# One more weight place, used once, ahead of the expert stages of a transformer kernel

## The reference, cut to what matters

```python
def second_block(x, mem, ...):
    h = x
    for layer in range(2):
        mix = mixer_ab(h, ...) if layer % 2 == 0 else mla(h, ...)
        h = layer_norm_2(DN_ALPHA * h + mix, ...)
        xa = mem_cross_attention(h, mem, xa_wq[layer], xa_wkv[layer], xa_wo[layer])
        h = layer_norm_2(DN_ALPHA * h + xa, ...)
        ff = hier_moe(h, ...)          # 32 experts in 4 groups, 2 chosen per token
        h = layer_norm_2(DN_ALPHA * h + ff, ...)
    return h

def expert_block(args):                # one block of rows of one expert e
    xb, e = args
    h = jax.nn.silu(xb @ w_gate[e]) * (xb @ w_up[e])   # 1024 -> 512
    return h @ w_down[e]                               # 512 -> 1024
```

## Time and profile before

| | |
|---|---|
| median of 3 runs | 2828.98 us (2827.93 to 2829.49) |
| profiled execution | 2828.16 us |
| its span | 2826.3 us, 38195 instructions |
| PE busy | 2510.8 us (89%), 16194 matmuls |
| DVE, ACT, POOL busy | 44%, 13%, 7% |
| DMA | 703.59 MB, mean 249 GB/s |
| mean granted TensorE clock | 0.952 |

### The profile page before, as it was taken

The page is one execution under the profiler, slowest core; times in us unless marked ns, Lnnn a source line. Parts: engine busy times, 40 slices in busy tenths (PEclk is TensorE's granted clock), DMA queues, the critical chain, the costliest instruction groups (busy, mean ns, idle before and its releaser), DMA issues.

```text
span 2826.3 us, 38195 instructions
## 1 busy us (share of the span) xinstructions
PE 2510.8 (89%) x16194; PEld 1656.4 (59%) x16194; DVE 1256.4 (44%) x2583; ACT 379.0 (13%) x865; POOL 210.5 (7%) x224
## 2 busy tenths in 40 slices
PE   9999999999999999999999999866667999756665
PEld 5779765796769947699457785322223675322221
DVE  4767664676666656777556532000002553000002
ACT  1410002100031001310022111000000412000000
POOL 0300012000120000400013000000000310000000
PEclk9999999999999999999999999988889999988888
DMA  8354543544535435254431868999999447999998
GB/s 322 120 161 156 190 145 120 189 157 161 193 106 178 176 116 205 89 190 170 143 128 49 297 244 343 421 421 421 421 421 386 182 185 304 421 421 421 421 422 340
DMA packets 245774, 703.59 MB, mean 249 GB/s; under 512 B 18795, under 2 KB 123753, under 8 KB 197219
## 3 DMA queue, kind: packets, MB, share of 16 engines
q1 hardware_dynamic: 244304, 699.30, 65.5%
q10 hardware_dynamic: 1299, 1.83, 0.2%
HBM read 698.20 MB, written 1.05 MB: 247 GB/s over the span
## 4 chain that ended last, share of the span: by engine, by line
PE 73%; DMA 21%; SPq 2%; ACT 2%; DVE 1%; issue 1%; DVEq 0%; ACTq 0%
PE lin L928 45%; PE sco L928 16%; PE trp L928 9%; DMA ring<-in_moe_w_down 5%; DMA ring<-in_moe_w_gate 5%; DMA arena<-in_moe_w_down 3%; DMA arena<-in_moe_w_up 2%; DMA arena<-in_moe_w_gate 2%; DMA ring<-in_moe_w_up 1%; PE trp L1097 1%; SPq L760 1%; DMA x<-in_moe_w_up 1%; DMA spare<-in_moe_w_gate 1%; PE trp L1193 1%; DMA x<-in_moe_w_down 1%
## 5 line engine op out<-in xcount | busy, mean ns | idle before, releaser
L928 PE MATMUL sco<-arena 128*32 128x512 f32 (+6 forms) x2560 | 551.5, 509 | 115.3 <-DMA ring<-in_moe_w_up 27.1
L928 PE MATMUL lin<-ring,arena 128*128 128x512 f32 (+3 forms) x1820 | 646.7, 504 | 2.6 <-DMA ring<-in_w_in_a 1.8
L928 PE MATMUL sco<-ring,arena 128*32 128x512 f32 (+2 forms) x1652 | 390.8, 690 | 136.6 <-DMA arena<-in_moe_w_up 39.2
L928 PEld LDWEIGHTS lin<-ring,arena 128*128 128x128 f32 x1820 | 339.0, 190 | 264.1 <-issue 238.6
L928 PEld LDWEIGHTS sco<-arena 128*32 128x32 f32 (+3 forms) x2560 | 201.5, 150 | 283.2 <-issue 271.2
L928 PE MATMUL lin<-arena 128*128 128x128 f32 (+8 forms) x2888 | 355.2, 300 | 3.6 <-ACT arena L2372 1.3
L3794 DVE TENSOR_TENSOR arena<-arena,sco 128x512 f32<-128x512 f32 x16 | 11.0, 687 | 758.1 <-PE sco L928 758.1
L928 PEld LDWEIGHTS lin<-arena 128*128 128x128 f32 (+3 forms) x2888 | 274.9, 170 | 63.1 <-issue 42.7
L928 PEld LDWEIGHTS sco<-ring,arena 128*32 128x32 f32 (+1 forms) x1652 | 107.3, 133 | 282.2 <-issue 275.3
L928 PE MATMUL trp<-arena 128*128 128x128 f32 (+2 forms) x1584 | 217.7, 292 | 1.3 <-ACT arena L2559 0.7
L2856 POOL TENSOR_TENSOR roots<-roots 128x1 f32<-128x1 f32 (+2 forms) x42 | 38.8, 926 | 2270.9 <-DVE roots L2981 2248.4
(11 more groups left out here) (366 smaller groups left out, 2369.1 us busy)
## 6 DMA issues: line engine op xcount, KB each, us to landing
ring<-in_w_gate_up SPq DMA_DIRECT2D x88, 1024.0 KB, 5.6
ring<-in_moe_w_up SPq DMA_DIRECT2D x66, 1024.0 KB, 26.7
ring<-in_moe_w_down SPq DMA_DIRECT2D x65, 1024.0 KB, 27.0
ring<-in_moe_w_gate SPq DMA_DIRECT2D x61, 1024.0 KB, 26.7
arena<-in_moe_w_gate SPq DMA_DIRECT2D x54, 1024.0 KB, 26.7
arena<-in_moe_w_up SPq DMA_DIRECT2D x51, 1024.0 KB, 26.5
arena<-in_moe_w_down SPq DMA_DIRECT2D x47, 1024.0 KB, 26.7
ring<-in_w_down SPq DMA_DIRECT2D x44, 1024.0 KB, 5.4
```

The costliest lines, as they stand in the source:

```text
L928: return nc.tensor.matmul(o, lhsT, rhs, start=start, stop=stop, skip_group_check=not one_group)
```

## The change

A further place, ONCE_PLACE, is used for a single piece in each expert stage, piece 7 (the last of the second four gate pieces of the first round). It consists of 1536 floats of the arena, over `pair_h`, `pair_hT` and more that is first written later in the first round, and of the 512 floats of the causal mask. In `expert_slots` it is put in at position 7, so every place behind it takes a piece one later. In `load_moe` it is loaded as two transfers into one semaphore, and out of order: directly ahead of the piece for TURNED_PLACE, with the same wait on `pv_full`. Behind layer 0's pieces the mask is loaded again from HBM (256 KB), and DVE waits for that ahead of the attention of the second layer. The unread products take the identity, repeated four times, as moving operand. Some of the router's tables move over `rowsT`, `hot` shares its place with `chosen`, and `gathering` and all that is behind it move; `moe_x` and the extra places start 32 floats further on, and the arena is 32 floats longer.

```diff
+ONCE_PIECE = 2 * TOGETHER - 1
...
+        once.insert(ONCE_PIECE, ONCE_PLACE)
         count = ROUNDS * PIECES + 2 * len(EARLY_MEMORY)
     else:
-        once = []
         cycle = (free + [MEMORY_PLACE] + oldest[0:4] + SUMS_PLACES + oldest[4:6] + [KEYS_PLACE, VALUES_PLACE, TURNED_PLACE] + oldest[6:10]
                  + [MIXED_PLACE] + oldest[10:11] + [COLUMNS_PLACE] + oldest[11:] + [X_PLACE])
+        once = cycle[:ONCE_PIECE] + [ONCE_PLACE] + cycle[ONCE_PIECE:]
...
+def load_order(slots):
+
+    order = [m for m in range(len(slots)) if m != ONCE_PIECE]
+    order.insert(order.index(slots.index(TURNED_PLACE)), ONCE_PIECE)
+    return order
...
-        ARENA = 25600
+        ARENA = 25632
...
-        PAIR = GATE + 512
+        PAIR = GATE + 288
         rowsT = at(PAIR, KD, P)
+        logits36 = at(PAIR, NT, GROUPS + EXPERTS)
...
+        once_rows = [at(PAIR + 1024 + 512 * n, 512) for n in range(3)] + [causal[:, :, :].rearrange("p t k -> p (t k)")]
-        gathering = at(PAIR + 2304, NT, P)
-        moe_x = at(PAIR + 2560, NT, 2, 4, P)
-        turned_rows = at(PAIR + 2560 + NT * D, SLOT)
+        gathering = at(PAIR + 2560, NT, P)
+        moe_x = at(PAIR + 2816, NT, 2, 4, P)
+        turned_rows = at(PAIR + 2816 + NT * D, SLOT)
...
-                for m, src in enumerate(sources()):
-                    s = slots[m]
+                matrices = list(sources())
+                for m in load_order(slots):
+                    s, src = slots[m], matrices[m]
...
-                    elif s == TURNED_PLACE or s == VALUES_PLACE and layer:
+                    elif s in (TURNED_PLACE, ONCE_PLACE) or s == VALUES_PLACE and layer:
                         sp.wait_ge(pv_full, 2 * XA_HEADS * (layer + 1))
+                    if s == ONCE_PLACE:
+                        sp.dma_start(at(PAIR + 1024, 3, 512), src[:, 0:3, :]).then_inc(slot_full[s], 16)
+                        sp.dma_start(once_rows[3], src[:, 3, :]).then_inc(slot_full[s], 16)
+                        continue
...
                 for s, dst, src in last_halves:
                     sp.dma_start(dst, src).then_inc(slot_full[s], 16)
+                if values_ahead(layer):
+                    sp.wait_ge(slots_used, before + ONCE_PIECE + 1)
+                    sp.dma_start(causal[:, :, :].rearrange("p t k -> p (t k)"), const("causal")).then_inc(causal_loaded, 16)
...
             def busy_work():
 
                 for n in range(4 + 2 + 1):
-                    mm(lin[:, 0, :], ident[:, :], causal[:, :, :].rearrange("p t k -> p (t k)"))
+                    mm(lin[:, 0, :], ident[:, :], ident[:, :].unsqueeze(1).to_broadcast([P, 4, P]))
...
                     for _ in range(TOGETHER):
                         s = next(next_slot)
+                        if s == ONCE_PLACE:
+                            pe.wait_ge(slot_full[s], full[s].next(32))
+                            parts.append(once_rows)
+                            continue
...
+                dve.wait_ge(causal_loaded, 16)
                 attend_pairs([causal] * (MLA_HEADS // 2), range(KD))
```

More of the change, by code:

```diff
@@ L69 @@
 (VALUES_PLACE, MEMORY_PLACE, KEYS_PLACE, X_PLACE, COLUMNS_PLACE, TURNED_PLACE,
- MIXED_PLACE) = [RING + EXPERT_EXTRA + n for n in range(7)]
+ MIXED_PLACE, ONCE_PLACE) = [RING + EXPERT_EXTRA + n for n in range(8)]
+ONCE_PIECE = 2 * TOGETHER - 1
 SUMS_PLACES = [RING + EXPERT_EXTRA - 2, RING + EXPERT_EXTRA - 1]
@@ L106, in expert_slots @@
     assert taken[MIXED_PLACE] < count - 2 * TOGETHER
+    assert taken[ONCE_PLACE] == ONCE_PIECE
     return places, earlier
+def load_order(slots):
+    order = [m for m in range(len(slots)) if m != ONCE_PIECE]
+    order.insert(order.index(slots.index(TURNED_PLACE)), ONCE_PIECE)
+    return order
 FFN_UNITS = D_FF // (2 * P)
@@ L317, in build @@
         late_row_sums = at(0, 2, 2, 512)
-        first_head_sums = at(ARENA - 880, 2, 3, P)
+        first_head_sums = at(ARENA - 912, 2, 3, P)
         mla_row_sums = at(14592, 8, 512)
@@ L347, in build @@
         chosen = at(GATE + 128, NT, COLUMNS)
+        hot = at(GATE + 128, NT, EXPERTS)
         numbers = at(GATE + 192, EXPERTS)
[L349 to L357, removed]
-        PAIR = GATE + 512
-        rowsT = at(PAIR, KD, P)
+        router = at(GATE + 224, NT, 16)
+        most = at(GATE + 256, 8)
+        PAIR = GATE + 288
+        rowsT = at(PAIR, KD, P)
+        logits36 = at(PAIR, NT, GROUPS + EXPERTS)
+        late_gates = at(PAIR, NT, EXPERTS)
+        picked = at(PAIR + 72, NT, GROUPS, PER_GROUP)
+        group_hot = at(PAIR + 136, NT, GROUPS)
+        group8 = at(PAIR + 144, NT, 8)
+        top8 = at(PAIR + 160, NT, 8)
+        group_exps = at(PAIR + 176, NT, GROUPS)
         pair_h = at(PAIR + 1024, MOE_FF)
@@ L364, in build @@
         spreadT = at(PAIR + 2048, NT, P)
-        gathering = at(PAIR + 2304, NT, P)
-        moe_x = at(PAIR + 2560, NT, 2, 4, P)
-        turned_rows = at(PAIR + 2560 + NT * D, SLOT)
+        once_rows = [at(PAIR + 1024 + 512 * n, 512) for n in range(3)] + [causal[:, :, :].rearrange("p t k -> p (t k)")]
+        gathering = at(PAIR + 2560, NT, P)
+        moe_x = at(PAIR + 2816, NT, 2, 4, P)
+        turned_rows = at(PAIR + 2816 + NT * D, SLOT)
         moe_sum = at(2048, NT, D)
-        EXTRA = PAIR + 2560 + NT * D + SLOT
+        EXTRA = PAIR + 2816 + NT * D + SLOT
         extra = at(EXTRA, EXPERT_EXTRA, SLOT)
@@ L459, in build @@
         sco = psum("sco", 2)
-        slot_full = [sem(f"slot_full{s}") for s in range(MIXED_PLACE + 1)]
+        slot_full = [sem(f"slot_full{s}") for s in range(ONCE_PLACE + 1)]
         slots_used = sem("slots_used")
@@ L491, in build @@
         x_ordered, columns_read = sem("x_ordered"), sem("columns_read")
+        causal_loaded = sem("causal_loaded")
         first_half_loaded = sem("first_half_loaded")
@@ L2004, in expert_parts @@
                         s = next(next_slot)
+                        if s == ONCE_PLACE:
+                            pe.wait_ge(slot_full[s], full[s].next(32))
+                            parts.append(once_rows)
+                            continue
                         pe.wait_ge(slot_full[s], full[s].next(16))
-                        parts.append(slot_rows(s).rearrange("p (k n) -> p k n", k=k))
+                        rows = slot_rows(s).rearrange("p (k n) -> p k n", k=k)
+                        parts.append([rows[:, j, :] for j in range(k)])
                     return parts
@@ L2042, in unread @@
                     for _ in range(n):
-                        mm(trp[:, 0, :], ident[:, :], causal[:, :, :].rearrange("p t k -> p (t k)"))
+                        mm(trp[:, 0, :], ident[:, :], ident[:, :].unsqueeze(1).to_broadcast([P, 4, P]))
                 def combine(n, i):
@@ L2076, in moe @@
                                 for r, wk in zip(expert_rows, parts):
-                                    last = mm(sco[r, gate_or_up, :], rowsT[:, 4 * half + k, r], wk[:, k, :],
+                                    last = mm(sco[r, gate_or_up, :], rowsT[:, 4 * half + k, r], wk[k],
                                               start=half + k == 0, stop=half == 1 and k == 3)
@@ L2100, in moe @@
                                 for r, wd in zip(expert_rows, parts):
-                                    last = mm(sco[r, n, :], pair_hT[:, 2 * half + f, r], wd[:, f, n * 512:(n + 1) * 512],
+                                    last = mm(sco[r, n, :], pair_hT[:, 2 * half + f, r], wd[f][:, n * 512:(n + 1) * 512],
                                               start=half + f == 0, stop=half + f == 2)
@@ L2666, in moe @@
                     act.wait_ge(vec_for_act, t_vec.next())
-                    nc.scalar.activation(hot[:, t, 0:GROUPS], logits36[:, t, 0:GROUPS], ACT.Exp, bias=router[:, t, 8:9],
+                    nc.scalar.activation(group_exps[:, t, :], logits36[:, t, 0:GROUPS], ACT.Exp, bias=router[:, t, 8:9],
                                          accum_out=router[:, t, 9:10])
```

## The result

The changed kernel takes 2813.44 us (median of 6 runs, 2811.46 to 2816.73), the one before 2829.23 (6 runs, 2825.44 to 2831.2): a ratio of 0.995, interval 0.9939 to 0.996. That is 15.8 us less (11 to 17 by the interval), where 5.0 were forecast. The profiled execution's span is 2809.6 us, 16.7 shorter.

The account below looks back on a forecast made before the run. Expert stages end paced by the 421 GB/s weight stream, the rest is PE-bound; -4.98 for the lead plus 0 each for mask, fillers and tables/arena/router takes 2828.98 to 2824.0 us, range 2822.2 to 2827.4.

Parts of the forecast that it names:

- The lead of one MB: Both expert stages: the new place puts one MB more ahead, so each ends 2.49 us earlier, -4.98 us in sum.
- B: Expert stages: one keeps its MB, the other gives it back as its queue runs dry once; 2826.5 us, chance 0.09.
- C: Expert stages: neither keeps its MB of lead; 2829.0 us, chance 0.04.
- D: Expert stages: a MB is worth more than the mean, 3.18 us at 330 GB/s; 2822.6 us, chance 0.11.
- The mask's load: Behind layer 0's stage: the 256 KB reload takes 0.68 us, within 1.9 us of slack; 0 taken, 0 to +0.9 kept.
- The fillers: Unread products ahead of layer 1's stage and in the tails: repeated identity as fast as the mask, 592 ns a pass; 0.
- E: Unread products: the repeated identity costs double, +7.7 us, so the kernel is slower at 2831.7 us; chance 0.05.
- Tables, arena, router ... I take 0: Router tables move with the same operations; expert buffers behind and spare start 128 bytes later, loads land alike; 0 us.
- Rival F: Stage loads into the arena: the 128-byte shift lowers their rate, 384 for 421 GB/s, +36.5 us; 2860.5 us, chance 0.04.

## Why the prediction was wrong, point by point

**The lead of one MB: right.** By the cuts of the stages, the changed kernel against the same without the place is 473.52 against 476.48 and 460.26 against 462.48: -2.96 and -2.22. The pair with all buffers moved is 471.29 against 474.04 and 459.37 against 461.33: -2.75 and -1.96. The mean over both pairs is -4.95 for both stages; -4.98 was worked out. The third pair, the kernel without the shift against before, gives -0.74 and -2.42, the first of them with the 1.6 us of a fallen clock in it. That neither stage gives it back was right too (rivals B and C are out). The shortest time from issue to landing behind the early memory products, named as the test, after and without the place:

```profile
DMA to landing us min/median/max: 9.5/10.6/11.6
```

```profile
DMA to landing us min/median/max: 12.0/13.0/14.1
```

2.5 us apart, the price of a MB, and still above the 5.6 of a lone load. (The forecast had 10.9 for the shortest, from the 13.4 of before.) A MB was worth its mean, so D is out as well.

**The mask's load: right.** The memory weights were issued at 2149.49, landed 11.8 us later at 2161.3, and PE read them at 2162.48: 1.2 us of slack, the 1.9 less the 0.68 worked out. DVE never waited for the mask; it landed 10.5 us after its issue at 2147.8, and its first reader starts at 2227.7.

**The fillers: right**, 592 ns a pass in the changed kernel too, so E is out:

```profile
L951 PE MATMUL lin<-ident x14: 592/592/676, 2361.3 to 2372.2; 128*128 128x512 f32 x14
```

**The step that failed is "Tables, arena, router ... I take 0".** The prediction saw that the places behind the gathered rows, and spare, move by 128 bytes, and priced it at nothing since loads into ring and arena "which start at different offsets, land alike". That comparison was worth nothing, for two reasons. First, by the count above, both buffers started 128 bytes past a multiple of 256, as did x and spare: there was no buffer of the other kind to compare with. An offset within the program is not an address in the partition; one must add up all that is allocated ahead of it. Second, 26 to 27 us from issue to landing in a full queue is the length of the queue, some ten transfers of others, and doesn't show the price of one's own. Even at 427 GB/s that median is 26.8 us within layer 0's stage, against 27.3 before. What the runs showed instead: the shift alone is worth 3.4 us in each stage, and 6.9 us in the median (0.9973).

Rival F named this very mechanism, with 0.04, but looked only at a loss. It also counted all 152 MB of loads into the arena, though those into mixT, xT and memT don't move and those into spare do. For a change of address, nothing in the trace excluded a gain, and the forecast gave no lower bound for it, as it did for the other unknowns. With -7 as that bound, the range would have reached down to 2817. The two effects' sum is -5.0 and -6.9, -11.9, which lies within the interval of the result and is close to the 12.2 us found in the stages. The 3.9 us from there to the median's -15.8 aren't shown by any run: against the before measured beside each, the kernel without the place is 8.4 us faster and the one without the shift 6.4, and the medians of before themselves lie between 2827.1 and 2829.2. They are likely scatter between executions.

**The mechanism of the address: open.** That the starts make the rate is shown, by moves alone. How they do isn't. Worked out from the traces' packet records, before rounding, the rates in GB/s of the two windows are these, beside what they would be if each place on a multiple of 256 gave its own share of the rise from 421.2 to 426.7 and 426.8:

| kernel | places on a multiple of 256, layers 0 and 1 | measured | by shares |
|---|---|---|---|
| before | 0 of 22, 0 of 25 | 421.2, 421.2 | |
| only spare moved (one run) | 0 of 22, 2 of 25 | 421.2, 422.1 | 421.2, 421.7 |
| nothing but the shift | 7 of 22, 9 of 25 | 424.3, 424.8 | 422.9, 423.2 |
| ring and x alone | 13 of 22, 13 of 25 | 426.5, 425.9 | 424.4, 424.1 |
| all moved | 22 of 22, 25 of 25 | 426.7, 426.8 | |

The gain is well above the share wherever only some places are moved. A move helps the loads of its neighbours in the stream too, or a start off the multiple costs more among others of its kind. "Each place by its own start", which stands in several expectations, is refuted.

The Trainium skill, "DMA: Bandwidth & Descriptors", section "How a descriptor splits into AXI transactions", says that each transaction into which a transfer is split, of 256 bytes or less, must start on a multiple of 256, and that the bytes between that boundary and the true start are fetched unused and cost beats of 32 bytes. Its table has small pieces only. By the rule a row of 8 KB costs 256 beats on a boundary and 260 from 128 bytes past one, 1.6% more: an estimate. In the mean these runs are near it: 426.7 against 421.2 is 1.3%. In the rest they don't agree. A start 64 past would cost 258 beats and one 192 past 262, so the far places would have moved the rate to some 422.3 and 420.1, both estimates; the runs have 421.1 to 421.2 for either. A count for each row gives plain shares, which the table above doesn't show. And it would lengthen every row: before, 4726 of the 18482 packets of 8192 bytes in layer 0's window took 309 ns, with a mean of 313.9, and with all moved 18697 of 18723 took 309 ns. The section speaks of bytes that are fetched, and here only the places that are written moved. The prediction weighed the same page's limit of the HBM and not this section; its estimate would have turned a zero into a term of the right sign.

## What to carry to other kernels

Where a stage runs at the full rate of its DMAs, look up the byte at which each buffer starts within the partition. Here a start on a multiple of 256 bytes for rows of 8 KB was worth 1.3% of the stream, for no instruction at all: 2828 to 2814 us with one unused line of 32 floats, about as much as the whole change, of which the new place alone gave some 5. One more buffer ahead of such a stage was worth its bytes over the stream's rate, and can be where it is filled while the queues are empty; check that with a hole in the DMA windows, and that it's kept with the shortest issue-to-landing time. And when an edit moves buffers as a side effect, build the move alone, or its gain is booked to the idea.

## What the runs showed of the hardware that I had not expected

The rate of the weight stream took these values, over 340 and 360 us: 421 GB/s with all places 128 bytes past a multiple of 256, or with the far ones at 64 or 192 past; 424 to 425 with 7 of 22 places (layer 0) or 9 of 25 (layer 1) on a multiple; 426 to 427 with ring and x on one; 427 with all. So a third of the places gave over half of the gain. The granted clock of TensorE can fall to the lower of its two levels for some 3.4 us (6.8 in one) with PE busy throughout (2196 to 2202 before, PE busy for all of the 10 us from 2186 too), which costs 1.7 us, and it does so at a few places of the program in some executions and not in others.
